# Moving the branch on further visits ahead of the last expert's down product, with copies in halves at both ends of the expert loop

## The reference

```python
logits = (x @ w_router + b_router).astype(f32)
top_v, top_i = lax.top_k(logits, TOP_K)                 # 4 of 32 experts
top_w = jax.nn.softmax(top_v, axis=-1)
gates = jnp.sum(jax.nn.one_hot(top_i, N_EXPERTS, dtype=f32) * top_w[..., None], axis=-2)
def expert_step(acc, ep):
    w1, b1, w2, b2, g = ep
    hdn = x @ w1 + b1
    gt = jnp.minimum(hdn[:, :D_FF], SWIGLU_LIMIT)
    up = jnp.clip(hdn[:, D_FF:], -SWIGLU_LIMIT, SWIGLU_LIMIT)
    act = (up + 1.0) * gt * jax.nn.sigmoid(SWIGLU_ALPHA * gt)
    return acc + g[:, None] * (act @ w2 + b2), None
...
gate = jax.nn.sigmoid(_rms_norm(h, lw['norm_ple']) @ lw['w_ple_gate'])
h = h + gate * (p_l @ lw['w_ple_proj'])
```

## Time and profile before

| | us |
|---|---|
| median of 3 runs | 1177.43 |
| lowest, highest | 1175.02, 1178.19 |
| profiled execution, its own time | 1176.99 |
| its span | 1174.9 |
| PE busy in the span | 1117.8 |
| DVE busy | 329.9 |
| ACT busy | 191.9 |
| share of the 16 engines that the main DMA queue's packets took | 86.9% |

### The profile page before, as it was taken

How to read it: one execution, slowest core, us unless ns; L and a number is a source line. 1 busy time by engine, 2 the same in 40 slices (tenths; PEclk the granted TensorE clock), 3 DMA queues, 4 the chain that set the end, 5 groups by cost and what they waited for, 6 DMA issues and landing times.

```text
span 1174.9 us, 14469 instructions
## 1 busy us (share of the span) xinstructions
PE 1117.8 (95%) x5723; PEld 474.9 (40%) x5723; DVE 329.9 (28%) x618; ACT 191.9 (16%) x367; POOL 94.4 (8%) x154
## 2 busy tenths in 40 slices
PE   4997999999999999999999999999999999999987
PEld 3664644333333333333434333333334333333356
DVE  6999434111222111211111111121111111111234
ACT  3144312111111111111111111111101111111132
POOL 5665000000000000000000000000000000000022
PEclk9996987999999999999999999999999999999999
DMA  9522625999999999999999999999999999999931
GB/s 277 200 60 125 227 62 192 430 428 427 427 428 426 428 427 428 428 428 428 428 427 428 426 427 427 428 427 428 428 426 387 416 412 426 428 427 428 425 153 38
DMA packets 45868, 426.38 MB, mean 363 GB/s; under 512 B 10992, under 2 KB 15216, under 8 KB 20960
## 3 DMA queue, kind: packets, MB, share of 16 engines
q1 hardware_dynamic: 45184, 425.06, 86.9%
q10 hardware_dynamic: 624, 0.45, 0.1%
HBM read 424.12 MB, written 2.41 MB: 363 GB/s over the span
## 4 chain that ended last, share of the span: by engine, by line
PE 79%; DMA 11%; DVE 6%; issue 1%; ACT 1%; ACTq 0%; SPq 0%; DVEq 0%
PE ps L1182 34%; PE ps L1203 16%; DMA ring_up<-in_w_up_dram 11%; PE ps L1105 5%; PE ps L1144 3%; PE ps L1488 2%; PE ps L1162 2%; PE ps L863 2%; PE ps L1195 2%; PE ps L1153 2%; PE ps L664 1%; DVE ps L2008 1%; PE ps L719 1%; PE ps L996 1%; PE ps L938 1%
## 5 line engine op out<-in xcount | busy, mean ns | idle before, releaser
L1182 PE MATMUL ps<-ring_up,region 128*64 128x512 f32 x2024 | 447.0, 597 | 6.1 <-DMA ring_up<-in_w_up_dram 5.4
L1182 PEld LDWEIGHTS ps<-ring_up,region 128*64 128x64 f32 x2024 | 142.5, 137 | 284.1 <-issue 272.6
L1203 PE MATMUL ps<-ring_dn,region 128*64 128x512 f32 x1024 | 234.0, 598 | 0.7 <-ACT region L1772 0.7
L2350 DVE TENSOR_SCALAR region<-ps 128x512 f32<-128x512 f32 (+1 forms) x33 | 22.6, 684 | 433.7 <-PE ps L1182 432.1
L1203 PEld LDWEIGHTS ps<-ring_dn,region 128*64 128x64 f32 x1024 | 68.2, 136 | 139.8 <-issue 111.3
L1768 ACT ACTIVATE region<-region 128x512 f32<-128x512 f32 x32 | 20.2, 631 | 459.2 <-DVE region L2350 459.2
L2342 DVE TENSOR_TENSOR fb<-fb,ps 128x528 f32<-128x528 f32 x64 | 45.1, 704 | 142.9 <-PE ps L1105 127.9
L606 POOL COPY region<-kst 128x64 f32 (+1 forms) x32 | 7.6, 238 | 944.1 <-PE ps L1182 855.6
L1105 PE MATMUL ps<-region 128*128 128x264 f32 x256 | 75.5, 414 | 1.8 <-DVE fb L2342 1.8
L1782 ACT ACTIVATE region<-ps 64x512 f32<-64x512 f32 x64 | 37.9, 592 | 220.3 <-PE ps L1203 219.9
L2331 DVE TENSOR_TENSOR region<-ps,g_xe 128x512 f32<-128x512 f32 x32 | 22.1, 692 | 169.9 <-PE ps L1153 169.9
(11 more groups left out here) (424 smaller groups left out, 871.4 us busy)
## 6 DMA issues: line engine op xcount, KB each, us to landing
ring_up<-in_w_up_dram SPq DMA_DIRECT2D x126, 2048.0 KB, 18.3
ring_dn<-in_w_down_dram SPq DMA_DIRECT2D x64, 2048.0 KB, 16.8
ring_up<-in_w_in_dram SPq DMA_DIRECT2D x4, 1024.0 KB, 9.8
ring_dn<-in_w_out_dram SPq DMA_DIRECT2D x1, 4096.0 KB
ring_up<-in_w_ple_gate_dram SPq DMA_DIRECT2D x4, 1024.0 KB, 19.6
x_tok<-in_x_prompt_dram SPq DMA_DIRECT2D x2, 512.0 KB
ring_up<-in_w_in_dram SPq DMA_DIRECT2D x2, 512.0 KB, 8.9
ring_up<-in_w_glu_dram SPq DMA_DIRECT2D x1, 1024.0 KB
```

The lines of the kernel that those rows point to most:

```text
L1182: m = mm(ps[64 * (q % 2):64 * (q % 2) + 64, HID_B + q // 2, :], xe[:, k % 4, k // 4], row[:, q * 512:(q + 1) * 512], start=False, stop=(k ...
L1203: m = mm(ps[64 * half:64 * half + 64, OUT_B, :], act_t[:, f % 4, 64 * (f // 4):64 * (f // 4) + 64], ring_dn[:, f, 512 * half:512 * half + ...
```

## The change

- `further_visits` is split: `each_visit` is its loop without the outer test. On SP, ACT and DVE nothing changes by this.
- On PE the last pair now ends behind its second up product: parts 2 and 3 of the pair before follow there one after the other, part 3 into banks 4 and 5 (`LAST_B`) and not banks 6 and 7. Then the count is read. If it is over 0, the last expert's turn, down product and `combine_pair` (`last_expert`) and the visits run. If it is under 1, a second copy of `last_expert` runs, and the tail follows.
- ACT's last `outputs` raises `dn_sb` behind each half. The last `combine_pair` waits for the first half ahead of part 0 and for the second ahead of part 2. The count in `visit` is one higher.
- DVE's first copy into `xe` is in two halves. The first raises `sel_early`, for which the first four rows of the first up product wait. The second raises `xe_rdy`.

```diff
@@ combine_pair (PE)
+                halves = last and p == PAIRS - 1
                 outputs = out_e[:, a].rearrange("p h n -> p (h n)")
                 for j in parts:
+                    if halves and j == 2:
+                        pe.wait_ge(Z["dn_sb"], 2 * p + 3 + s)
@@ up (PE)
-                pe.wait_ge(Z["xe_rdy"], u + 1)
+                pe.wait_ge(*((Z["sel_early"], 3) if isinstance(u, int) and u == 0 and UP - 1 not in ks else (Z["xe_rdy"], u + 1)))
@@ pair (PE), place "last"
                 if place == "last":
+                    combine_pair(p - 1, 1 - a, s, (3,), last=True)
                     n_visits = visits_listed(pe)
+                    return
@@
+            def last_expert():
+
+                pe.wait_ge(Z["gt_sb"], PAIRS + 1)
+                turn_activations(NE)
+                down(NE - 1, NE)
+                combine_pair(PAIRS - 1, 1, 1, last=True)
+
@@ behind the last quad (PE)
-            combine_pair(PAIRS - 1, 1, 1, last=True)
-            further_visits(pe, n_visits, visit)
+            with pe.If(n_visits > 0):
+                last_expert()
+                each_visit(pe, n_visits, visit)
+            with pe.If(n_visits < 1):
+                last_expert()
@@ outputs (ACT)
                 for half in range(2):
                     m = f(out_e[C * half_:C * half_ + C, a, half], ps[64 * half:64 * half + 64, OUT_B], ACT.Copy)
-                m.then_inc(Z["dn_sb"], 1)
+                    if last or half == 1:
+                        m.then_inc(Z["dn_sb"], 1)
@@ added(p - 1, (3,)) in DVE's pair: banks of LAST_B at place "last"
-                    added(p - 1, (3,))
+                    added(p - 1, (3,), place == "last")
@@ ahead of the quads (DVE)
-            gathered(0)
+            dve.wait_ge(Z["xt_ps"], 1)
+            for h in range(2):
+                V.tensor_tensor(xe[:, :, h], ps[:, XT_B].rearrange("p (i h s) -> p i h s", i=4, h=2)[:, :, h],
+                                g_cols[:, :, h].unsqueeze(2).to_broadcast([P, 4, C]), ALU.mult
+                                ).then_inc(*((Z["sel_early"], 1) if h == 0 else (Z["xe_rdy"], 1)))
```

More of the change, by code:

```diff
@@ L363, in visits_listed, with each_visit @@
             return eng.value_load(vis_int[0:1, VISITS:VISITS + 1], min_val=0, max_val=VISITS)
+        def each_visit(eng, n, body, expert_of=False):
+            with eng.Fori(1, VISITS) as v:
+                with eng.If(n >= v):
+                    body(v, eng.value_load(vis_int[0:1, bass.ds(v - 1, 1)], min_val=0, max_val=NE - 1)
+                         if expert_of else None)
+                eng.nop()
         def further_visits(eng, n, body, expert_of=False):
             with eng.If(n > 0):
[L368 to L372, removed]
+                each_visit(eng, n, body, expert_of)
         @block.sync
@@ L1399, in pair @@
                 if place == "last":
+                    combine_pair(p - 1, 1 - a, s, (3,), last=True)
                     n_visits = visits_listed(pe)
+                    return
                 pe.wait_ge(Z["gt_sb"], p + 1 + s)
                 turn_activations(u + 1)
-                if place != "last":
-                    bias_and_samples(t + 2, 0)
+                bias_and_samples(t + 2, 0)
                 if place == "visit":
@@ L1409, in pair @@
                     down(t + 1, u + 1, FIRST)
-                    if place != "last":
-                        turn_gathered(u + 2)
+                    turn_gathered(u + 2)
                     if place == "embed":
@@ L1442, in visit @@
                 turn_selection(PAIRS + v)
-                pe.wait_ge(Z["dn_sb"], u + 1)
+                pe.wait_ge(Z["dn_sb"], u + 2)
                 pe.wait_ge(Z["gt_sb"], PAIRS + 1 + v)
@@ L1776, in selection, with outputs @@
                 f(g_t[:, a], bank(TURN_B, T), ACT.Copy).then_inc(Z["gt_sb"], 1)
-            def outputs(t, a, half_):
+            def outputs(t, a, half_, last=False):
                 act.wait_ge(Z["dn_free"], DN * t + DN)
@@ L1840, in pair @@
                     visit_activation(u + 2)
-                outputs(u + 1, a, 1)
+                outputs(u + 1, a, 1, place == "last")
                 if place == "visit":
```

## The result

| | before | changed |
|---|---|---|
| median of 20 runs, us | 1179.63 | 1172.51 |
| lowest, highest | 1175.02, 1181.54 | 1168.75, 1175.48 |
| ratio, 95% interval | | 0.9949 [0.9938, 0.9961] |
| profiled execution, its own time | 1176.99 | 1174.26 |
| its span | 1174.9 | 1172.3 |

The change is faster by 6.0 us (4.6 to 7.3, by the interval of the ratio). But the gain forecast was 3.9 us, the two profiled executions differ by only 2.6 us of span, and neither end of the loop went as predicted. The median before is now 1179.63, where the forecast started from three runs at 1177.43. These figures for one change have to be brought together.

What follows compares the result with a forecast made beforehand. PE and the DMA engines were both near their limit in the expert loop, leaving its start and end; 1.19 + 2.52 + 0.2 = 3.9 us took the profiled 1176.99 to 1173.1, median 1173.5. Range 1171.2 to 1176.8 us.

Steps and rivals of the forecast that it cites:

- The second half of the outputs: Kernel's end: the last pair's part 0 waits for ACT's first half copy alone and starts 1.19 us earlier.
- The branch at its old place: Behind the last part: with PE's branch gone, the tail's product follows without a hole, 2.52 us gained.
- The near branch at the join: Behind the last part: unconditional branch to the next instruction, 50 to 62 ns, hidden; rival that it fetches too, 0.06.
- The branch at its new place: Ahead of the last turn: 3.40 us, up to 4.1 under DMA load, hidden by PE's wait for DVE; cost 0.
- the cover is too short: Rival at the last turn: branch takes 5.5 to 6.5 us, turn 1 to 2 us late, 1174.5 to 1175.5; chance 0.13.
- Code waits in line like weights: Rival at the last turn: code request waits 19.6 us as weights do, turn 17.4 us late, 1190.9 us; chance 0.04.
- The first half of `xe`: Loop's start: first up product starts 0.27 us earlier, behind DVE's first half copy; taken as 0.2 us.
- the rise stays: Loop's start: PE's rise to 2.4 GHz stays where it is, so the 0.27 us gained are worth 0.135.
- it moves along: Loop's start: PE's clock rise moves along with the earlier start, so the gain is worth 0.27 us.
- the rise that comes earlier: Rival at the loop's start: clock rise comes forward by more than the work, 1.8 us more gained, 1171.7; chance 0.05.

Runs made afterwards that it cites:

- the halves alone: Kernel before with part 3 ahead of the last turn and the last outputs copied and awaited in halves, branch at its old place; ratio 0.9973, 3.2 us.
- the two second profiles: The kernel before and the changed kernel, each run again with no edit; ratios to before 0.9996 and 0.9955.
- the straight one: Changed kernel with the no-visits case first and a second copy of the tail, so PE reaches the tail without a jump; ratio to before 0.9928, median 1170.92 us.

## Why the prediction was right, and where it was wrong

The direction and the range held. The gain was 6.0 us and not 3.9, and the sum met it only roughly, since two terms were wrong in opposite directions and a third was missing. That the median came within 1.0 us of the forecast is luck in part: the three runs before had their median 2.2 us below that of the twenty. From 1179.63 the same sum gives 1175.7, which is 3.2 us too high, though still in the range.

- **The second half of the outputs**, -1.19: right, -1.29. Part 0 starts where it was put, and the four parts keep their length. The experiment with the halves alone shows the same.
- **The branch at its old place**, -2.52: right, -2.59. There is no hole, and L1493 follows o = 0 at once. The near branch at the join costs nothing that shows.
- **The branch at its new place**, 0: wrong. The step that failed is its price. I took 3.40 us from a row with idle DMA engines and added 0.12 + 0.62 for the load. Measured are 6.1 and 6.3 us; under load in other places 6.0 to 6.5. The rival "the cover is too short", 0.13, had the right size, 5.5 to 6.5 us, and the right lateness, 1 to 2 us. The cover itself was computed right: the branch started at 1110.4, 1.8 us before part 2, and 4.8 us of it were hidden. The packet itself took 1.10 us, as priced; what I had wrong is the wait before it, 3.6 us and not 1.0 + 0.62. "Code waits in line like weights" fell: 3.6 us are not 19.6.
- **The first half of `xe`**, -0.2: wrong in size. It is 0.27 and 1.4 to 1.6 more, since the clock rises earlier. The term stood between two bounds, "the rise stays" and "it moves along"; the rise that comes earlier was a rival, with 0.05 and a price of 1.8 us more. That is what all five profiles with halves show. The gain passed through the waits for weights, as said: the last up product still has it.
- **The base**: missing. The sum was made against an execution without the drop of the clock at the tail's product, which five of the seven profiles with the hole have and none of the seven without it. The same first profile also had no drop in the down product, which costs 1.69 us in the comparison of the first profiles and nothing in that of the second ones.

With the two second profiles the sum closes. From part 2 to the end of the span the kernel before takes 1178.3 - 1113.95 = 64.35 us in its second profile, and the change 1173.3 - 1112.85 = 60.45 in its own, 3.9 less. Both have the drop in the down product. The loop is 918.63 against 917.01, 1.6 less, and the start 0.27. That is 5.8 us, where the runs say 6.0 (4.6 to 7.3). The spans of these two differ by 5.0, since the work ahead of the loop took 0.8 us longer in the changed kernel's. The 1.6 to 1.9 us that the turn lost are in the 5.8: they are what a version without the jump gets back (3.1 us for the one without visit code, run beside the changed kernel; 2.5 for the straight one, by ratios whose intervals overlap).

## What to carry to other kernels

Don't let the common case jump over a large body of code. Put the rare case behind it, so that the common one falls through, and look at the end of the kernel too, where a jump over the rare case stood beside a last wait 1.6 us longer. If a far jump must be, price it at the load of the place where it will stand, not of the place where it stood. Where TensorE has short pauses just ahead of a long stretch of matmuls, look at the granted clock of its first microseconds: filling two pauses of 0.7 and 0.8 us there was worth 2.5 us. And take a second profile before a sum in single microseconds: two executions of one kernel differed by 3.4 us in span, nearly all of it in two places.

## What the runs showed of the hardware

- A taken branch over 137 matmul calls or more took PE 3.3 to 3.7 us with idle DMA engines (nine jumps) and 6.0 to 6.5 us with full ones (seven jumps, in four kernels). The code packet takes about as long in both (0.9 to 1.2 and 1.0 to 1.1 us); it starts 1.0 us behind the branch when they are idle and 3.5 to 4.0 when they are full.
- The Trainium skill, "Runtime: NRT & Kernel Launch", section "Instruction fetch mechanics", says that a taken branch out of the fetched window forces a fetch. The trace agrees: a 16 KB packet of the instruction queue moved in each of the 16 jumps. The section also gives PE a store of 2048 instructions. The 137 calls are some 550, an estimate from the two matmul and two weight-load records that a call leaves here, and that jump was fetched for each time. Whether the store is smaller or just isn't filled that far ahead, no run here tells.
- PE's sequencer ran about 3.5 us ahead of its matmuls at the loop's end (1110.7 against 1114.16), which hides that much of a branch.
- The clock fell to 1.2 GHz inside the dense last down product in ten of 14 profiles, which cost 1.4 to 1.7 us each time. PE's pause ahead of the turn was 0.95 to 2.8 us in the ten. It was 0.95 to 1.84 us in three of the other four, so its length doesn't decide alone.
